# Merging the short-convolution branch before the conformer branch, and reordering VectorE's and ScalarE's work around attention

## What is computed

```python
def conformer_conv(glu_in, dw, dw_b, ln_g, ln_b, w_out):
    a, g = jnp.split(glu_in, 2, axis=-1)
    u = depthwise_conv(a * jax.nn.sigmoid(g), dw) + dw_b      # width 31
    u = jax.nn.silu(layer_norm(u, ln_g, ln_b))
    return u @ w_out

def short_conv(sc_in, dw, w_out):
    bg, cg, xin = jnp.split(sc_in, 3, axis=-1)
    return (bg * depthwise_conv(cg * xin, dw)) @ w_out        # width 3

def merge_branches(gate_in, y_att, y_conv, y_sc, w_o):
    g_att, g_conv, g_sc = jnp.split(jax.nn.sigmoid(gate_in), N_BRANCH, axis=-1)
    return (g_att * y_att + g_conv * y_conv + g_sc * y_sc) @ w_o

# in each layer
h = modulate(rms_norm(x, ln1_g[l]), sh1, sc1)
proj = h @ w_in[l]
...
x = x + g1 * merge_branches(proj[..., SC_END:GATE_END], att, y_conv, y_sc, w_o[l])
h2 = modulate(rms_norm(x, ln2_g[l]), sh2, sc2)
x = x + g2 * swiglu(h2, w_ff1[l], w_ff3[l], w_ff2[l])
```

## Time and profile before

| what | value |
|---|---|
| runs | 1418.75, 1419.19, 1421.95 us; median 1419.19 |
| the profiled execution | 1419.28 us, its span 1417.5 us |
| TensorE matmuls | 1279.1 us busy, 90% of the span |
| TensorE weight loads (beside matmuls) | 1037.9 us, 73% |
| VectorE | 693.6 us, 49% |
| ScalarE | 534.2 us, 38% |
| GpSimd | 399.3 us, 28% |
| read from HBM | 185.49 MB, 132 GB/s |
| a load of 512 KB of input-projection weights, issue to landing | 4.0 us, median of 78 |

### The profile page before, as it was taken

One profiled execution on the slowest core, in us unless ns is written; L12 is line 12 of the kernel. 1 busy time (PEld: TensorE's weight loads), 2 busy tenths in 40 slices (PEclk: granted clock), 3 DMA queues, 4 the chain that ended last, 5 costly groups with the idle time before them and its releaser, 6 DMA issues. The chain is left out here.

```text
span 1417.5 us, 20637 instructions
## 1 busy us (share of the span) xinstructions
PE 1279.1 (90%) x7166; PEld 1037.9 (73%) x7166; DVE 693.6 (49%) x1069; ACT 534.2 (38%) x875; POOL 399.3 (28%) x234
## 2 busy tenths in 40 slices
PE   4699987779999979999999999979988987899997
PEld 1467665557777757778777877758766887899996
DVE  1545566676344455322332233378678444744444
ACT  2342434333222334232222123345555443544443
POOL 3141201011121242222122212524322355244444
PEclk9699999999999989999999999989999998899998
DMA  8456311112645233563456345525332574466652
GB/s 291 140 179 185 85 46 47 43 49 55 189 145 174 76 116 119 178 178 119 121 177 188 109 128 173 152 65 141 84 96 69 134 189 143 115 199 178 179 167 70
DMA packets 275192, 187.52 MB, mean 132 GB/s; under 512 B 12540, under 2 KB 261682, under 8 KB 275122
## 3 DMA queue, kind: packets, MB, share of 16 engines
q1 hardware_dynamic: 275121, 186.57, 44.9%
HBM read 185.49 MB, written 1.05 MB: 132 GB/s over the span
## 5 line engine op out<-in xcount | busy, mean ns | idle before, releaser
L312 POOL TENSOR_TENSOR Wlo<-Wraw,Whi 128x1024 fp32r<-128x1024 f32 (+4 forms) x165 | 329.4, 2003 | 881.0 <-ACT Whi L301 879.9
L1388 PE MATMUL bank<-Hhi,Whi 128*128 128x256 f32 (+2 forms) x1200 | 411.0, 343 | 6.2 <-POOL Wlo L312 3.1
L1390 PE MATMUL bank<-Hhi,Wlo 128*128 128x256 f32 (+2 forms) x1200 | 404.9, 337 | 0.0
L1389 PE MATMUL bank<-Hlo,Whi 128*128 128x256 f32 (+2 forms) x1200 | 404.8, 337 | 0.0
L301 ACT ACTIVATE Whi<-Wraw 128x1024 fp32r<-128x1024 f32 (+4 forms) x330 | 277.8, 863 | 260.9 <-PE bank L1390 107.6
L312 DVE TENSOR_TENSOR Wlo<-Wraw,Whi 128x1024 fp32r<-128x1024 f32 (+3 forms) x165 | 182.2, 1114 | 190.8 <-ACT Whi L301 190.2
L1388 PEld LDWEIGHTS bank<-Hhi,Whi 128*128 128x128 f32 (+1 forms) x1200 | 227.5, 190 | 56.1 <-issue 29.8
L1390 PEld LDWEIGHTS bank<-Hhi,Wlo 128*128 128x128 f32 (+1 forms) x1200 | 227.4, 189 | 25.2
L1389 PEld LDWEIGHTS bank<-Hlo,Whi 128*128 128x128 f32 (+1 forms) x1200 | 227.6, 190 | 24.3 <-issue 0.7
L1388 PE MATMUL bank<-Uhi,Whi 128*128 128x512 f32 (+1 forms) x480 | 164.6, 343 | 0.9 <-POOL Wlo L312 0.8
L1389 PE MATMUL bank<-Ulo,Whi 128*128 128x512 f32 (+1 forms) x480 | 162.6, 339 | 0.0
(11 more groups left out here) (135 smaller groups left out, 1441.3 us busy)
## 6 DMA issues: line engine op xcount, KB each, us to landing
Wraw<-in_w_ff SPq DMA_DIRECT2D x120, 512.0 KB, 4.6
Wraw<-in_w_in SPq DMA_DIRECT2D x78, 512.0 KB, 4.0
ATT<-in_w_mod SPq DMA_DIRECT2D x72, 512.0 KB, 4.6
ACC<-in_w_mod SPq DMA_DIRECT2D x20, 512.0 KB, 6.6
Wraw<-in_w_o SPq DMA_DIRECT2D x16, 512.0 KB, 4.7
Wraw<-in_w_ff SPq DMA_DIRECT2D x16, 384.0 KB, 4.4
Wraw<-in_w_mla_o SPq DMA_DIRECT2D x8, 512.0 KB, 3.4
Wraw<-in_w_kv_b SPq DMA_DIRECT2D x12, 256.0 KB, 3.6
```

The lines of the kernel that those rows point to most:

```text
L312: last = eng.tensor_tensor(lo, raw, hi.bitcast(F32), ALU.subtract)
L1388: pe.matmul(dst, sh, mh, start=j == 0, stop=False)
L1389: pe.matmul(dst, sh, ml, start=False, stop=False)
L1390: last = pe.matmul(dst, sl, mh, start=False, stop=j == k - 1)
```

## The change

- **Values after keys and queries.** SyncE loads, ScalarE empties, and TensorE and VectorE work off the first pair's keys and queries before the values product. The modulation rows that VectorE added before the first rotation are added after it.
- **Pairs.** They are unrolled. ScalarE does both heads' copies and then both exponentials, where it took them in turn; the gate's tanh and the next weight split come after duo NS-1 (the second in layer 0, the first in layer 1) instead of after the first. VectorE splits its weights after the maxima of duo NS.
- **Taps.** Of the 28 taps after the first three, each pair has 3 in layer 0 and 4 in layer 1; the output product has 6 and 4, the first two branch groups 5 and 5, or 4 and 4.
- **Output product.** Nothing lies between its tiles but the taps.
- **Branches.** Eight groups of two gate tiles and two branch tiles: four of the short convolution, then four of the conformer. The conformer's bias comes after group 1, its mean after the first gate tile of group 2, its squares and root in group 3, and its scaling and tanh at the end of that. It works in ACC and SQ instead of Z and TG. SyncE waits for the last "attended" before it loads the first branch weights, and no longer for the end of the normalisation.
- **First tiles.** An operand tile's two products with its high part wait for the high part only; the product with the low part follows a step later. Each high part of W_o's operand waits for its own bank's two sums.

```diff
-TAPS_BEFORE, TAPS_PER_PAIR = 3, 7
+TAPS_BEFORE = 3
+TAPS_IN_PAIR = [3, 4]
+TAPS_IN_OUTPUT = [[1, 1, 2, 2], [1, 1, 1, 1]]
+TAPS_IN_GROUP = [[5, 5], [4, 4]]
...
-HEAD_KINDS = ["values", "keys", "queries"]
+HEAD_KINDS = ["keys", "queries", "values"]
...
-        values()
         keys(0)
         queries(0)
+        values()
...
+        if l == 0:
+            sp.wait_ge(pv_done, len(duos_of(0)) * PAIRS)
+        for b, w in ((2, w_sc_o), (1, w_conv_o)):
+            with at.loop(sp, 2, chunks=8, mods=4 if l == 0 else 0) as i:
+                for g in range(2):
+                    for j in range(2):
+                        load(wi, 0, DT, i * (4 * CW) + (GATE0 + b * D + (2 * g + j) * CW), CW)
+                    for j in range(2):
+                        load(w[l], 0, 2, i * (4 * CW) + (2 * g + j) * CW, CW)
+                    if l == 0:
+                        for j in range(2):
+                            mod(0, 2, i * 2 + (8 - 4 * b + g), j, "branches")
...
+        act.wait_ge(sq_summed, at.square.now())
+        for t in product:
+            act.wait_ge(drained[t.bank], t.drained)
+        for tt in range(4):
+            copy_out(V[:, tt, :])
...
-            for _ in exps(0):
-                pass
+            exps(0)
             look(next(looks))
             gate_a = at.tile()
             for d in range(len(duos) - 1):
-                for _ in zip(copies(d), exps(d + 1)):
-                    pass
-                if d == 0:
+                copies(d)
+                exps(d + 1)
+                if d == NS[l] - 1:
                     gate_out(gate_a, p * 2)
                     look(next(looks))
...
-            for _ in copies(len(duos) - 1):
-                pass
+            copies(len(duos) - 1)
...
+        for m in range(4):
+            for _ in range(2):
+                at.tile()
+            if m < 3:
+                look(next(nxt))
+        outs = []
+        def group(first_done=None):
+            before = outs[-2:]
+            for j in range(2):
+                look(next(nxt))
+                if before:
+                    act.wait_ge(drained[before[j].bank], before[j].drained)
+                copy_out(TG[:, j, 0:TQ], TQ, ACT.Tanh, 0.5)
+                if j == 0 and first_done:
+                    first_done()
+            for j in range(2):
+                look(next(nxt))
+                outs.append(at.tile())
...
+        def mean_squares():
+            mean = at.tile()
+            act.wait_ge(drained[mean.bank], mean.drained)
+            for j in range(2):
+                last = act.activation(SQ[:, j, 0:TQ], ACC[:, j, 0:TQ], ACT.Square)
+            last.then_inc(conv_sq, 1)
...
+        def normalised():
+            act.wait_ge(conv_v, l + 1)
+            for j in range(2):
+                last = act.activation(SQ[:, j, 0:TQ], ACC[:, j, 0:TQ], ACT.Tanh, scale=0.5)
+            last.then_inc(conv_t, 1)
+            act.wait_ge(conv_s, l + 1)
...
             for d in range(1, len(duos)):
                 soften(d)
+                if d == NS[l]:
+                    look(next(looks))
                 if d < 3:
                     do_taps(1)
-                if d == 1:
-                    look(next(looks))
             if not last:
                 at.tile()
                 rope_queries()
                 look(next(looks))
-                do_taps(1)
                 look(next(looks))
-            for w in taps:
-                tap(p * (2 * TAPS_PER_PAIR) + (CDW + 2 * w), p * TAPS_PER_PAIR + w)
+            do_taps(TAPS_IN_PAIR[l] - min(len(duos), 3))
...
         look(next(nxt))
+        for j in range(2):
+            low(Ulo[:, SO0 + j, 0:TQ], BG[:, j, 0:TQ], Uhi[:, SO0 + j, 0:TQ])
+        for m in range(4):
+            attended(2 * m)
+            attended(2 * m + 1)
+            if m < 3:
+                look(next(nxt))
+            do_taps(TAPS_IN_OUTPUT[l][m])
+        settle()
+        dve.wait_ge(q_ready, at.heads.now())
+        outs = []
+        def group(i, taps=0, first_done=None):
+            gates, before = [], outs[-2:]
+            for j in range(2):
+                look(next(nxt))
+                gates.append(at.tile())
+                if j == 0 and first_done:
+                    first_done()
+                do_taps(max(0, min(2, taps - 2 * j)))
+            for j in range(2):
+                look(next(nxt))
+                t = full()
+                dve.wait_ge(drained[gates[j].bank], gates[j].drained)
+                if before:
+                    dve.wait_ge(drained[before[j].bank], before[j].drained)
+                mark(dve.scalar_tensor_tensor(Z[:, j, 0:TQ], TG[:, j, 0:TQ], 1.0,
+                                              banks[t.bank][:, 0:TQ], add, mult))
+                after_all()
+                if j:
+                    through(outs[-1])
+                dve.tensor_tensor(G[:, i * 2 + j, 0:TQ], G[:, i * 2 + j, 0:TQ], Z[:, j, 0:TQ],
+                                  add).then_inc(drained[t.bank], 1)
+                outs.append(t)
+            do_taps(max(0, taps - 4))
...
+        def scaled():
+            take_root(TQ, stat_root(l, 3))
...
+        group(0, TAPS_IN_GROUP[l][0])
+        group(1, TAPS_IN_GROUP[l][1])
         after_all()
...
+        group(2, first_done=centred)
+        group(3, first_done=scaled)
...
+        for i in range(4):
+            group(i)
...
+        for j in range(DT + 1):
+            if j < DT:
+                pe.wait_ge(op_hi, ready + j + 1)
+                for t, slot, n in zip(tiles, slots, ns):
+                    w, dst = slice(j * P, (j + 1) * P), banks[t.bank][:, 0:n]
+                    pe.matmul(dst, Whi[:, slot, w], Hhi[:, j, 0:n], start=j == 0, stop=False)
+                    pe.matmul(dst, Wlo[:, slot, w], Hhi[:, j, 0:n], start=False, stop=False)
+            if j:
+                pe.wait_ge(op_lo, ready + j)
+                for t, slot, n in zip(tiles, slots, ns):
+                    w, dst = slice((j - 1) * P, j * P), banks[t.bank][:, 0:n]
+                    last = pe.matmul(dst, Whi[:, slot, w], Hlo[:, j - 1, 0:n], start=False, stop=j == DT)
+                    if j == DT:
+                        last.then_inc(tile_done, 1)
...
+        pe.wait_ge(op_lo, at.operand.n - 3)
+        keys = keys_tile()
+        pe.wait_ge(op_lo, at.operand.n)
+        slot = chunk()
+        for h in range(2):
+            query_tile(h, slot)
         slot, vt = chunk(), []
         for tt in range(4):
...
-        pe.wait_ge(conv_a, l + 1)
-        over_channels(ACC)
-        mla()
-        pe.wait_ge(conv_sq, l + 1)
-        over_channels(SQ)
-        mla()
-        mla()
-        at.operand.n += 4
...
+        for _ in range(3):
+            mla()
+        def group(o0, first_done=None):
+            for j in range(2):
+                tile_of(P, DT, H, 0, TQ)
+                if j == 0 and first_done:
+                    first_done()
+            pe.wait_ge(op_lo, at.operand.n)
+            for j in range(2):
+                tile_of(P, 2, O, o0, TQ)
             if l == 0:
...
+        at.operand.n += 2
+        group(SO0)
+        group(SO0)
+        group(SO0, mean_over_channels)
+        group(SO0, squares_over_channels)
+        at.operand.n += 2
+        for _ in range(4):
+            group(CO0)
```

259 lines of the change are left out of this document (72 added, 187 removed).

## The result

The changed kernel takes 1357.86 us (median of four runs, 1356.93 to 1359.93), the kernel before on the same chip 1418.97. The ratio is 0.9567, with a 95% interval of 0.955 to 0.9585: faster by 61 us, where the prediction said 53 and gave 1355 to 1384 as its range. The profiled execution has a span of 1355.6.

The account below looks back on a forecast made before the run. It took TensorE's idle time, mostly attention's waits for copies and probabilities, as what could be won. Terms -37.4 - 6 - 2.9 - 3.25 - 2.7 - 5.7 + 4.6 = -53.35 against 1419.28 gave 1366 us, range 1355 to 1384.

Parts of the forecast that it names:

- Attention's waits: Attention pairs: copies ahead of exponentials and fewer taps remove all but 3.0 of 40.4 us of TensorE waits, -37.4 us.
- keys first: Start of attention: the 3.8 us wait for rotated queries goes, small waits for value copies are new, -2.9 us.
- The clock: Attention matmuls behind waits run at the lower clock level; this partly ends, -6 us, between nothing and -9.8.
- First tiles: Phase starts: TensorE needs only high parts first, -3.25 us at four places; -2.7 us at the two output projections.
- Output product: Conformer moved behind the short convolution: two waits for VectorE's G and four short ones go, -5.7 us.
- New waits in the groups: Layer 1's branch groups: waits for channel mean and for weight splits behind the root and normalised branch, +4.6 us, 0 to 12.
- the clock that stays low: Rival: remaining short waits keep the clock at its lower level in places, 1372 us; chance included in the forecast's 0.66.
- VectorE's debt: Rival: in branch groups 0 to 4, locked taps and bank emptying delay scaling and mean, 1381 us; chance 0.16.
- ScalarE's queue: Rival: branch-stage weight splits come late behind waits for VectorE, TensorE stops once a group, 1424 us; slower, chance 0.03.
- The pairs did shorten: Rival said they would not: exponentials behind both copies delay the next transposes, half of 37.4 stays, 1385 us; chance 0.08.
- the rule that was weighed: Two-SBUF-input VectorE operations and GpSimd ones take the port in turn, each for its whole instruction; spoke against taps in groups.

Follow-up runs that it names:

- the first experiment: Changed kernel with ScalarE again taking copy, exponential, copy, exponential in turn, taps left as changed: 1383.58 us beside 1420.06 for the kernel before (ratio 0.9747).

## Why the prediction was right

By its own steps, which are these:

- **Attention's waits, -37.4, and keys first, -2.9**: 38.1 of idle time went, where the two terms make 40.3. Its mechanism holds in its main parts: with the copies' order undone "attended" waits 17.5 us, with the taps put back "probsT" 14.9, with values first the scores 3.8. Of the gate's tanh and split it is half right: by their place alone only the 1.44 returns, and the 1.03 needs the old order too. What it expected to stay (0.3 twice a pair) is 0.34 and 0.25. New waits for probabilities it did not see are 0.56 and 1.15, in the fourth pairs. Pairs take 29.8 us where it said 31, and 17.4 where it said 18. Keys first brought 4.4 rather than 2.9, but only with the clock: the idle part is 2.1, since the wait for the value copies is 1.6 and not 0.9.
- **The clock, -6: the term that was mis-sized.** The busy time fell by 15.8. The step that failed is the count: it took the 26 + 30 gate, key and query matmuls that the timeline lists singly, and even its bound of 9.8 left out scores, transposes and "attended". What it counted gave back 7.8 (6.4 and 1.4 in the two layers), within its bounds; what it left out gave back 8.5 more (5.7 and 2.8). Grouped by shape over layer 0's attention, us busy and mean ns, in the kernel before:

```profile
L1564 PE MATMUL bank<-Hlo,Whi 128*128 128x512 f32 x64 | 26.7, 418 | 0.0
...
L1600 PE MATMUL attended<-ATT,V 128*64 128x128 f32 x192 | 17.4, 328 | 16.4 <-ACT ATT L759 16.4
L1580 PE MATMUL scores<-ATT 96*128 96x512 f32 x32 | 17.3, 638 | 1.5 <-DVE ATT L1161 1.5
```

And in the kernel after:

```profile
L1571 PE MATMUL bank<-Hlo,Whi 128*128 128x512 f32 x64 | 25.0, 391 | 0.0
...
L1587 PE MATMUL scores<-ATT 96*128 96x512 f32 x32 | 15.8, 595 | 0.6 <-ACT V L591 0.6
L1607 PE MATMUL attended<-ATT,V 128*64 128x128 f32 x192 | 14.0, 281 | 1.2 <-ACT ATT L763 1.0
```

  "Attended" gives back 3.4 us, and it comes right behind the wait. The granted clock in the earlier trace rows said as much: 0.92 over a stage of 152 us is some 12 us for that layer alone, and 11.7 were measured.
- **First tiles, -3.25 and -2.7**: the experiment gives 5.9 us of idle time for 5.95, of which 0.9 in layer 1 comes back as later waits for GpSimd. The norms gave 0.9 and 0.5 at half width, as said (7.38 to 6.47 at the one of the earlier trace rows). At layer 0's output projection the edit gives 1.87 for 2.0, but from before to after only 1.0 went (3.30 to 2.28): TensorE comes to it earlier, since the last branch group ends with one modulation step instead of two, and with the steps in pairs the wait is 1.4. The stage's clock was 0.92 for 0.89 in the profiled execution, and in another one 0.89.
- **Output product, -5.7**: as said; layer 0's idle 1.5 and layer 1's 4.2 are gone.
- **New waits in the groups, +4.6**: layer 1's idle time in the groups grew from 1.9 to 5.4, by 3.5, with the two longest where the prediction had put them, 1.27 for the channel mean and 1.77 for a GpSimd split behind the normalised branch. Layer 0's groups wait for nothing, but are 1.1 longer by busy time. That is a cost I did not count: the modulation steps, which the diff takes apart from pairs into single ones, 1.4 by the experiment that puts them together. The sum, 4.6, is exactly what was predicted, and partly by luck, since 1.1 of it is this other cost.
- **Rivals**: the clock that stays low did not happen, it came back wholly. VectorE's debt costs 0.9 at one place, the wait for the channel mean (1.27, and 0.35 without taps in the groups); GpSimd's waits are the same without them. ScalarE's queue costs at one place in layer 1, 1.77 us and not in every group. The pairs did shorten.

On the rule that was weighed, from the Trainium skill (SBUF — State Buffer, "SBUF: two separate sides"): this trace shows it at work again, a tap of 3.50 beside GpSimd's 2.56 at 169.91, with the pair of halves ending at 173.41, 0.55 after the split's end at 172.86. But these late taps cost TensorE nothing once no copy stands behind their maxima. With the order undone (the rows of the first experiment), "attended" waits 2.18 us behind the same tap, where the duos without a late maximum wait 0.4 to 0.8.

In all the forecast was 8 us too cautious: 9.8 by the clock term, less 1.7 by the others and by what lies between executions. The time lies near the lower end of the range; the mechanism was right, and one term was less than half of what was measured.

## What to carry to other kernels

When an in-order engine serves two chains, put the instruction whose input is ready ahead of the one that waits for another engine; here that alone was 24 us, without removing the delay itself (most of it at the places where the other engine was late). Work with slack belongs where the bound engine has long uninterrupted stretches, not between a result and the engine that waits for it. And price a lower clock by the whole stage, its length times what the granted clock lacks (15.6 for the 15.8 measured in the two stages of attention; 8.0 for 7.8 in layer 0 with the order undone), not by the slow matmuls one happens to see, since any form behind the wait can pay.

## What the runs showed of the hardware

- In attention, 38.1 us less idle time came with 15.8 us less busy time, two fifths of it again, as the granted clock rose from 0.92 and 0.96 to 1.00. The share is not fixed: with the copies' order undone, the twelve waits before "attended" in layer 0 (13.7 us) came with 7.8 more busy time, the four in layer 1 (3.8 us) with 0.2; the granted clock was 0.94 and 1.00.
- Behind W_o's wait in layer 0 the granted clock of the stage was 0.89 or 0.92 with a wait of 2.3 in two executions of the same kernel, and 0.95 with one of 1.4 in each of the three kernels that had it. The stage's length moves by 1.6 us with it, so that single executions can't tell apart edits of that size.
- A modulation step, four small matmuls between streams of full ones, costs 1.19 us, two together 2.05: here what is small was better taken in one place.
- A table load on ScalarE takes 1.28 us in the changed kernel too, once for the root and once for the tanh behind it.
